# Most gate and up tiles of a feed-forward layer computed with the weights stationary and x moving

## What is computed

```python
def swiglu(x, w_gate, w_up, w_down):
    return (jax.nn.silu(x @ w_gate) * (x @ w_up)) @ w_down

x = layer_norm(alpha * x + 0.5 * swiglu(x, ffn_w_gate[l, 0], ffn_w_up[l, 0], ffn_w_down[l, 0]),
               ln_g[l, 0], ln_b[l, 0])
...
h = h + 0.5 * _swiglu(_rmsnorm(h, ffn_norm[layer, 0]), ffn_w_gate_up[layer, 0], ffn_w_down[layer, 0])
```

## Time and profile before

| | us |
|---|---|
| median of 3 runs (lowest, highest) | 1726.74 (1725.92, 1729.38) |
| the profiled execution | 1726.31 |
| its span, first to last instruction | 1724.6 |
| PE busy in it | 1666.2 |
| DVE busy | 966.6 |
| ACT busy | 746.5 |

### The profile page before, as it was taken

One profiled execution on the slowest core, in us unless ns is written; L12 is line 12 of the kernel. 1 busy time (PEld: TensorE's weight loads), 2 busy tenths in 40 slices (PEclk: granted clock), 3 DMA queues, 4 the chain that ended last, 5 costly groups with the idle time before them and its releaser, 6 DMA issues.

```text
span 1724.6 us, 19555 instructions
## 1 busy us (share of the span) xinstructions
PE 1666.2 (97%) x8230; PEld 1393.8 (81%) x8230; DVE 966.6 (56%) x1016; ACT 746.5 (43%) x910; POOL 32.5 (2%) x53
## 2 busy tenths in 40 slices
PE   7999999998999999999999999997999989999998
PEld 6888888877788877888898888886888877888887
DVE  5555556867755546555467555464655454555552
ACT  5534344646344424444344444343544343535441
POOL 0000000000000000000000000000000020000000
PEclk9999999989999999999999999998999986999999
DMA  8565483434466555555465665454665450037551
GB/s 270 176 215 196 134 265 126 135 93 140 146 220 200 203 177 164 177 202 191 141 228 161 196 188 198 165 174 156 209 193 196 164 171 1 1 109 223 182 194 73
DMA packets 226087, 291.11 MB, mean 169 GB/s; under 512 B 10516, under 2 KB 203728, under 8 KB 225872
## 3 DMA queue, kind: packets, MB, share of 16 engines
q1 hardware_dynamic: 226000, 289.87, 51.1%
HBM read 288.78 MB, written 1.05 MB: 168 GB/s over the span
## 4 chain that ended last, share of the span: by engine, by line
PE 81%; DVE 9%; ACT 3%; issue 2%; DMA 2%; POOL 1%; SPq 0%; DVEq 0%; POOLq 0%; ACTq 0%
PE bank L1532 24%; PE bank L1534 24%; PE bank L1533 24%; DVE w_lo L979 3%; PE bank L1991 2%; PE bank L1693 2%; ACT w_hi L637 1%; PE bank L1541 1%; PE bank L2016 1%; POOL stats L582 1%; DVE z_sb L1041 1%; DVE x_sb L1012 1%; PE bank L2001 1%; DMA raw<-in_w_in_dram 1%; DVE bn L1019 0%
## 5 line engine op out<-in xcount | busy, mean ns | idle before, releaser
L979 DVE TENSOR_TENSOR w_lo<-raw,w_hi 128x2048 fp32r<-128x2048 f32 (+1 forms) x268 | 607.9, 2274 | 335.0 <-ACT w_hi L637 333.8
L637 ACT ACTIVATE w_hi<-raw 128x2048 fp32r<-128x2048 f32 (+1 forms) x268 | 507.7, 1901 | 194.5 <-DMA raw<-in_ffn_w_down_dram 97.2
L1532 PE MATMUL bank<-w_hi,xT_lo 128*128 128x512 f32 (+1 forms) x1360 | 541.2, 398 | 16.9 <-DVE w_lo L979 7.2
L1534 PE MATMUL bank<-w_hi,xT_hi 128*128 128x512 f32 (+1 forms) x1360 | 532.2, 391 | 0.0
L1533 PE MATMUL bank<-w_lo,xT_hi 128*128 128x512 f32 (+1 forms) x1360 | 531.6, 391 | 0.0
L1532 PEld LDWEIGHTS bank<-w_hi,xT_lo 128*128 128x128 f32 x1360 | 258.5, 190 | 70.5 <-issue 10.2
L1534 PEld LDWEIGHTS bank<-w_hi,xT_hi 128*128 128x128 f32 x1360 | 258.0, 190 | 54.4
L1533 PEld LDWEIGHTS bank<-w_lo,xT_hi 128*128 128x128 f32 x1360 | 258.7, 190 | 50.2
L1532 PE MATMUL bank<-w_hi,hT_lo 128*128 128x512 f32 x528 | 206.4, 391 | 0.0
L1534 PE MATMUL bank<-w_hi,hT_hi 128*128 128x512 f32 x528 | 205.6, 389 | 0.0
L1533 PE MATMUL bank<-w_lo,hT_hi 128*128 128x512 f32 x528 | 205.4, 389 | 0.0
(11 more groups left out here) (249 smaller groups left out, 1248.5 us busy)
## 6 DMA issues: line engine op xcount, KB each, us to landing
raw<-in_ffn_w_gate_up_dram SPq DMA_DIRECT2D x176, 512.0 KB, 4.9
raw<-in_ffn_w_down_dram SPq DMA_DIRECT2D x132, 512.0 KB, 4.0
raw<-in_ffn_w_gate_dram SPq DMA_DIRECT2D x44, 512.0 KB, 4.0
raw<-in_ffn_w_up_dram SPq DMA_DIRECT2D x44, 512.0 KB, 5.0
raw<-in_w_in_dram SPq DMA_DIRECT2D x44, 512.0 KB, 4.9
raw<-in_conv_w_in_dram SPq DMA_DIRECT2D x24, 512.0 KB, 4.7
raw<-in_kv_w_dram SPq DMA_DIRECT2D x12, 512.0 KB, 4.3
raw<-in_w_out_dram SPq DMA_DIRECT2D x8, 512.0 KB, 3.6
```

The source lines that it names most:

```text
L637: nc.scalar.activation(w_hi[:, slot, 0:width], raw[:, slot, 0:width], ACT.Copy).then_inc(high_ready, 1)
L979: nc.vector.tensor_tensor(w_lo[:, slot, 0:width], raw[:, slot, 0:width], w_hi[:, slot, 0:width].bitcast(F32), ALU.subtract).then_inc(low_r ...
L1532: nc.tensor.matmul(o, x_lo, wh, start=first, stop=False, skip_group_check=shared)
L1534: return nc.tensor.matmul(o, x_hi, wh, start=False, stop=last_one, skip_group_check=shared)
```

## The change

In the first three tiles (phases 0 and 7) or two tiles (other phases) of each feed-forward layer nothing but places and banks changes. In the other 8 or 9 tiles the roles of the operands are exchanged. `xT_hi` and `xT_lo` become the two halves of one tensor `xT`, so that for each chunk both parts of x are 512 adjacent columns. `features(j, kh)` first runs 16 matmuls of 512 columns (4 chunks x 4 blocks of 128 features) with a high weight stationary and both parts of x moving, after a wait on `high_ready`; then 16 matmuls of 256 columns with a low weight stationary and the high part of x moving, after a wait on `low_ready`. The four blocks (two gate, two up) have a bank each, four banks a tile, by turns. A bank's left half collects x_hi by w_hi and w_lo, its right half x_lo by w_hi. The two halves are joined outside PE: ACT copies the right halves into `silu` and `h` (four copies of 128x256), DVE adds the left halves (four adds). ACT takes Silu in place (one instruction of 512 columns), DVE multiplies (one of 512), ACT writes `hT_hi` and DVE `hT_lo`, both from `h`, which already has features on the partitions. There is no `hidden` for these tiles. PE waits on `up_joined` for its banks.

Tensors and helpers:

```diff
-xT_hi = sb("xT_hi", [P, KC, S], F32R)
-xT_lo = sb("xT_lo", [P, KC, S], F32R)
+xT = sb("xT", [P, KC, 2, S], F32R)
+xT_hi, xT_lo = xT[:, :, 0, :], xT[:, :, 1, :]
...
+FEATURES = [[bank[i] for i in (0, 1, 4, 5)], [bank[i] for i in (2, 3, 6, 7)]]
...
+def token_tiles(n):
+    return 3 if n == 0 or behind_kv(n) else 2
+token_before = [sum(token_tiles(m) for m in range(n) if phases[m] == FFN) for n in range(len(phases))]
+joined_before = [FT * ffn_number[n] - token_before[n] for n in range(len(phases))]
+def hidden_bank(n, j):
+    return bank[4 + j % 2] if token_tiles(n) == 3 else bank[6 + j]
```

ACT:

```diff
-    act.wait_ge(hT_psum, FT * f + j + 1)
+    act.wait_ge(hT_psum, token_before[n] + j + 1)
     nc.scalar.activation(hT_hi[:, 2 * j:2 * j + 2, :],
-                         bank[4 + j % 2][:].rearrange("p (c m) -> p c m", c=2),
+                         hidden_bank(n, j)[:].rearrange("p (c m) -> p c m", c=2),
                          ACT.Copy).then_inc(hT_high, 1)
+def feature_tile(j):
+    before, done = FT * f + j, joined_before[n] + j - token_tiles(n)
+    split_to(s0 + 2 * j + LEAD)
+    act.wait_ge(slab_used, s0 + 2 * j + 2)
+    act.wait_ge(h_ready, 2 * before)
+    for fb in range(2):
+        nc.scalar.activation(silu[:, fb, :], FEATURES[j % 2][fb][:, S:2 * S], ACT.Copy).then_inc(low_half, 1)
+    act.wait_ge(hT_ready, before)
+    for fb in range(2):
+        nc.scalar.activation(h[:, fb, :], FEATURES[j % 2][2 + fb][:, S:2 * S], ACT.Copy).then_inc(low_half, 1)
+    split_to(s0 + 2 * j + 1 + LEAD)
+    act.wait_ge(gate_joined, done + 1)
+    nc.scalar.activation(silu[:], silu[:], ACT.Silu).then_inc(silu_ready, 2)
+    act.wait_ge(h_ready, 2 * before + 2)
+    nc.scalar.activation(hT_hi[:, 2 * j:2 * j + 2, :], h[:], ACT.Copy).then_inc(hT_high, 1)
 def tile(j):
-    if j > 0:
+    if 0 < j <= token_tiles(n):
         hidden(j - 1)
+    if j >= token_tiles(n):
+        feature_tile(j)
+        return
     split_to(s0 + 2 * j + LEAD)
     act.wait_ge(slab_used, s0 + 2 * j + 2)
...
     tile(j)
 for d in range(FC // 2):
-    if d == 1:
-        hidden(FT - 1)
```

DVE:

```diff
 evacuate_input(0)
 split_to(LEAD - 1)
-def small_parameters():
+def small_columns():
     dve.wait_ge(cols_psum, 1)
     nc.vector.tensor_copy(cols[:, 0:ROWS], bank[7][:, 0:ROWS]).then_inc(cols_ready, 1)
     dve.wait_ge(cols_ready, 1)
+def small_parameters():
...
     nc.vector.tensor_tensor(hT_lo[:, 2 * j:2 * j + 2, :],
-                            bank[4 + j % 2][:].rearrange("p (c m) -> p c m", c=2),
+                            hidden_bank(n, j)[:].rearrange("p (c m) -> p c m", c=2),
                             hT_hi[:, 2 * j:2 * j + 2, :].bitcast(F32),
                             ALU.subtract).then_inc(hT_ready, 1)
+def feature_tile(j):
+    done = joined_before[n] + j - token_tiles(n)
+    split_to(s0 + 2 * j + LEAD)
+    for fb in range(4):
+        part, joined = ((silu, gate_joined), (h, up_joined))[fb // 2]
+        dve.wait_ge(low_half, 4 * done + fb + 1)
+        ins = nc.vector.tensor_tensor(part[:, fb % 2, :], FEATURES[j % 2][fb][:, 0:S], part[:, fb % 2, :], ALU.add)
+        if fb % 2 == 1:
+            ins.then_inc(joined, 1)
+    dve.wait_ge(up_joined, done + 1)
+    dve.wait_ge(silu_ready, 2 * FT * f + 2 * j + 2)
+    nc.vector.tensor_tensor(h[:], silu[:], h[:], ALU.mult).then_inc(h_ready, 2)
+    dve.wait_ge(hT_high, FT * f + j + 1)
+    nc.vector.tensor_tensor(hT_lo[:, 2 * j:2 * j + 2, :], h[:], hT_hi[:, 2 * j:2 * j + 2, :].bitcast(F32),
+                            ALU.subtract).then_inc(hT_ready, 1)
+    split_to(s0 + 2 * j + 1 + LEAD)
 def tile(j):
-    if j > 0:
+    if 0 < j <= token_tiles(n):
         hidden(j - 1)
+    if j >= token_tiles(n):
+        feature_tile(j)
+        return
     split_to(s0 + 2 * j + LEAD)
+    if behind_kv(n) and j == 2:
+        keys_out(1, 6)
     for tt in range(NT):
         dve.wait_ge(silu_ready, 2 * FT * f + 2 * j + tt + 1)
...
 if n == 0:
     small_parameters()
 for j in range(3, FT):
     tile(j)
 for d in range(FC // 2):
-    if d == 1:
-        hidden(FT - 1)
     if d < FC // 2 - tail(n):
```

PE:

```diff
         pe.wait_ge(hT_ready, FT * f + j - 1)
-    dst = bank[4 + j % 2][:].rearrange("p (c m) -> p c m", c=2)
+    dst = hidden_bank(n, j)[:].rearrange("p (c m) -> p c m", c=2)
     for c in range(2):
         for tt in range(NT):
             ins = nc.tensor.transpose(dst[:, c, tt * P:(tt + 1) * P], h[:, tt, c * P:(c + 1) * P], ident[:])
     ins.then_inc(hT_psum, 1)
+def features(j, kh):
+    k = s0 + 2 * j + kh
+    hi, lo = slab_view(k % SLOTS, 4, 512)
+    pe.wait_ge(high_ready, k + 1)
+    for c in range(4):
+        x = xT[:, 4 * kh + c, :, :].rearrange("p a m -> p (a m)")
+        for fb in range(4):
+            at, o = slice(fb * P, (fb + 1) * P), FEATURES[j % 2][fb]
+            nc.tensor.matmul(o[:], hi[:, c, at], x, start=kh == 0 and c == 0, stop=False, skip_group_check=True)
+    pe.wait_ge(low_ready, k + 1)
+    for c in range(4):
+        for fb in range(4):
+            at, o = slice(fb * P, (fb + 1) * P), FEATURES[j % 2][fb]
+            ins = nc.tensor.matmul(o[:, 0:S], lo[:, c, at], xT_hi[:, 4 * kh + c, :], start=False,
+                                   stop=kh == 1 and c == 3, skip_group_check=True)
+    ins.then_inc(slab_used, 1)
 def tile(j):
-    gate_up(j, 0)
-    hidden(j - 1)
-    gate_up(j, 1)
+    turned = token_tiles(n)
+    if j < turned:
+        gate_up(j, 0)
+        hidden(j - 1)
+        if behind_kv(n) and j == 2:
+            pe.wait_ge(cmp_ready, 2)
+            transpose_keys(1, 6)
+        gate_up(j, 1)
+        return
+    if j == turned + 1:
+        pe.wait_ge(hT_ready, FT * f + j - 1)
+    if j >= turned + 2:
+        pe.wait_ge(up_joined, joined_before[n] + j - turned - 1)
+    if j == 3 and n == 0:
+        pe.wait_ge(cols_ready, 1)
+    if j == 3 and behind_kv(n):
+        pe.wait_ge(keys_ready, 2)
+    features(j, 0)
+    if j == turned:
+        hidden(j - 1)
+    features(j, 1)
...
-    if behind_kv(n) and j == 2:
-        pe.wait_ge(cmp_ready, 2)
-        transpose_keys(1, 6)
-if n == 0:
-    pe.wait_ge(loaded_rows, 16 * 9)
-    nc.tensor.transpose(bank[7][:, 0:ROWS], z_sb[0:ROWS, 0, 0:P], ident[0:ROWS, 0:ROWS]).then_inc(cols_psum, 1)
+    if n == 0 and j == 1:
+        pe.wait_ge(loaded_rows, 16 * 9)
+        nc.tensor.transpose(bank[7][:, 0:ROWS], z_sb[0:ROWS, 0, 0:P], ident[0:ROWS, 0:ROWS]).then_inc(cols_psum, 1)
 for j in range(3, FT):
     tile(j)
-if n == 0:
-    pe.wait_ge(cols_ready, 1)
-if behind_kv(n):
-    pe.wait_ge(keys_ready, 2)
-project(n, s0 + 2 * FT, FC // 2, hT_hi, hT_lo, lambda d: pe.wait_ge(hT_ready, FT * f + d + 1),
-        behind_first=lambda: hidden(FT - 1))
+pe.wait_ge(up_joined, joined_before[n] + FT - 1 - token_tiles(n))
```

More of the change, by code:

```diff
@@ L268, in two_block_kernel @@
         hT_psum = sem("hT_psum")
+        low_half = sem("low_half")
+        gate_joined = sem("gate_joined")
+        up_joined = sem("up_joined")
         hT_high = sem("hT_high")
@@ L1514, in _ @@
                             keys_out(0, 7)
-                        if behind_kv(n) and j == 2:
-                            keys_out(1, 6)
+                        if n == 0 and j == 1:
+                            small_columns()
                     if n == 0:
@@ L1735, in _ @@
                             transpose_keys(0, 7)
-                        if behind_kv(n) and j == 2:
-                            pe.wait_ge(cmp_ready, 2)
-                            transpose_keys(1, 6)
-                    if n == 0:
-                        pe.wait_ge(loaded_rows, 16 * 9)
-                        nc.tensor.transpose(bank[7][:, 0:ROWS], z_sb[0:ROWS, 0, 0:P], ident[0:ROWS, 0:ROWS]).then_inc(cols_psum, 1)
+                        if n == 0 and j == 1:
+                            pe.wait_ge(loaded_rows, 16 * 9)
+                            nc.tensor.transpose(bank[7][:, 0:ROWS], z_sb[0:ROWS, 0, 0:P], ident[0:ROWS, 0:ROWS]).then_inc(cols_psum, 1)
                     for j in range(3, FT):
                         tile(j)
-                    if n == 0:
-                        pe.wait_ge(cols_ready, 1)
-                    if behind_kv(n):
-                        pe.wait_ge(keys_ready, 2)
-                    project(n, s0 + 2 * FT, FC // 2, hT_hi, hT_lo, lambda d: pe.wait_ge(hT_ready, FT * f + d + 1),
-                            behind_first=lambda: hidden(FT - 1))
+                    pe.wait_ge(up_joined, joined_before[n] + FT - 1 - token_tiles(n))
+                    project(n, s0 + 2 * FT, FC // 2, hT_hi, hT_lo, lambda d: pe.wait_ge(hT_ready, FT * f + d + 1))
                 if kind == MIXER:
```

## The result

| | before | after |
|---|---|---|
| median (lowest to highest), 15 executions each | 1727.06 (1724.69 to 1732.94) | 1720.81 (1709.18 to 1726.76) |
| the profiled execution | 1726.31 | 1713.39 |
| its span | 1724.6 | 1711.7 |
| its mean granted clock | 0.976 | 0.977 |

The change makes the kernel faster: after takes 0.9949 of the time of before, 95% interval 0.9933 to 0.9964. The medians are 6.3 us apart; the forecast was 11.0, for a time of 1715.7 in a range of 1709 to 1724.

A forecast was written before the change was run, and what follows sets the result against it. The prediction took PE to bound the kernel in the gate and up part: -25.0 for transposes, +10.9 for longer slabs, +3.1 for changes of form, -11.0 in all. That gave a median of 1715.7 us, range 1709 to 1724.

The forecast's parts named there:

- The bound: Gate and up part of the FFNs: a microsecond of PE work is a microsecond of time, and nothing else is.
- Removed transposes: Turned gate and up tiles lose the four `hidden` transposes: 52 x 0.48 = 25.0 us saved on PE.
- The longer slab: Each of 104 turned slabs has eight more matmuls and loads, 5.545 against 5.440 us: 10.9 us added.
- the change of form: Going from 256-column to 512-column matmuls, once per turned slab, costs 0.03 us: 104 x 0.03 = 3.1 us added.
- Rival B: Turned slabs: no cost for going from 256 to 512 columns, so -14.1 us, 1712.6; chance 0.20.
- The sum: Over 52 turned tiles: -25.0 + 10.9 + 3.1 = -11.0 us, 0.21 per tile, period 11.15.
- The waits at nothing: PE's new or moved waits, and the phase 7 transposes moved into tile 2, stay hidden: taken as nothing.
- DVE's chain: In a turned tile, from ACT's first copy to DVE's last split: +10.3 us, inside 11.15 with 0.85 over.
- Rival D: Turned tiles: DVE's chain takes PE's place; at 13.5 us a tile, 57 us more, 1773; chance 0.04.
- Rival F: Turned slabs: weight loads using all rows stand in the open, 832 more costing 158 us, 1863; chance 0.01.
- Rival E: Clock behind PE's pauses: half-clock stretches of about 3.5 us; three more give 1726, one fewer 1712; chance 0.08 against gain.

The follow-up runs named there:

- r2_by_chunk: Changed kernel with high and low weight passes alternating chunk by chunk in each slab, PE waiting for the low part ahead of the slab: 1718.17 us, ratio 0.9944.
- r4_longer_dve_chain: Changed kernel with an unused DVE reduction of 2048 columns ahead of each low part in a turned tile, two a tile: 1753.79 us, ratio 1.016.
- r9_more_filled: Changed kernel with constant matmuls in three PE pauses plus three more groups (26 at the start, 12 and 8 later): 1708.79 us, ratio 0.9888.
- r6_look: Changed kernel as it is, one more profiled execution: 1712.5 us at a mean clock of 0.976.
- r8: Kernel before with three groups of constant matmuls in PE's pauses, its new gate and up form left out: 1712.22 us, ratio 0.9903.
- r10: Kernel before with three groups of constant matmuls in PE's pauses, the kernel of r8 once more: 1713.29 us, ratio 0.9914.
- r7_fill_pauses: Changed kernel with constant matmuls in three PE pauses (16, 28 and 16), results unused: 1700.45 us, ratio 0.9845.
- r11_after_filled_pair: The kernel of r7_fill_pauses once more, on one chip with the kernel of r10: 1698.72 us, ratio 0.983.

## Why the prediction was right, and where it was off

**The bound.** PE alone set the time in the gate and up part, before and after. Right: the chain of after holds nothing but PE, and its gain is there in all six layers.

**Removed transposes, 0.48 each time, 25.0 us.** Right to 3%: put back, they cost 0.465 in the chain, 24.2 us, and 24.7 over the six layers.

**The longer slab, 10.9 us, and the change of form, 3.1 us.** A slab was forecast at 5.545 + 0.03 = 5.575 and takes 5.565. The pitches read in the key and value phase held in this mix. The change of form costs 0.02 rather than 0.03 (r2_by_chunk). Together 13.0 us instead of 14.0. That it is not zero, as Rival B had it, is shown by r2_by_chunk; B's sum (-14.1) puts the profiled execution at 1712.2, nevertheless nearer to the 1713.39 than the forecast's 1715.3.

**The sum.** -11.0 forecast, -12.2 in the layers, -12.9 in the span. With the two added terms at 13.0 instead of 14.0 the sum is -12.0, which nearly closes the difference; with the transposes at the 24.2 or 24.7 that they cost when put back it is -11.2 or -11.7, so up to 1 us of the layers' gain stays unassigned. The profiled execution was forecast at 1715.3 and took 1713.39.

**The waits at nothing.** Right: `up_joined`, `cols_ready`, `keys_ready` and the transposes moved in phase 7 show nowhere among PE's waits.

**DVE's chain.** The forecast of +10.3 was right (+10.14), but Rival D's condition was wrong: it took the length of a chain with waits in it for DVE's period. Had DVE been the bound, most of those waits would have gone, and r4_longer_dve_chain shows 8.1 us of need a tile. D was further off than the 0.85 us of room suggested, and its price was too high for the lengthening tried: two reductions cost 41 us, not 137.

**The page's rule (Rival F).** A load of 190 ns stands in the trace for each of 3328 matmuls of the turned tiles, half of them with 256 columns, and none is in the open: the low pass takes 1.91 for sixteen loads and matmuls. The rule stands in the Trainium skill, "TensorE: Matmul & The Clock Gate", in the section "The mechanism", not in the one that the prediction names: a load overlaps matmuls in flight only if the row group differs. Every load here uses all rows, and this case's traces disagree with the rule in that form. The same section also names a load into a background weight buffer as one that is pulled ahead, which the prediction left out; the traces fit that, but no run here shows such a buffer.

**The clock (Rival E, 0.08).** Here the prediction was off. It gave one stretch of half clock more or less as 1712 to 1719, and the median came out 5.1 us above the forecast; 10 of 15 executions had a mean clock lower by about 0.006 and were about 8 us longer. Run again, the same kernel was in the shorter group in 7 of 8. None of the 15 executions lies between 1714.24 and 1718.36, where the forecast of 1715.7 stood: the median is inside the range because the range took in part of E, which is luck as far as the sum goes, and the chance of E was too small. That stretches of half clock begin behind pauses of PE is shown for those in the traces. Where the longer executions have theirs stays open: no profile fell on one.

## What to carry to other kernels

Where PE is the bound, price a new order by the distance from start to start of the same instruction form elsewhere in the trace, and count each change of form once; three such terms gave the gain in the six layers to 10%. To judge whether an engine behind PE takes over, do not take the length of its chain for its need: its waits for a third engine shrink when it is late (here from 2.94 to 0.89 us a tile). And look at the clock behind each pause of PE: constant matmuls in three pauses gave as much as the whole change did, and beside it, but each group must stand in a pause or it costs its own length (2.6 us for the twelve of r9_more_filled).

## What the runs showed of the hardware that was not expected

**The clock falls behind the same pause in one execution and not in another.** In after, PE pauses for 1.88 us ahead of a layer's input, and then its matmuls start 0.43 apart for a while:

```profile
455.51 1.87 PE L1596 MATMUL bank<-ident,x_sb 128*128 128x128 f32 x8 [1.88 <-DVE x_sb L1064]
457.03 0.78 PE L1587 MATMUL bank<-w_hi,xT 128*128 128x512 f32 x1
457.60 0.63 PE L1588 MATMUL bank<-w_lo,xT 128*128 128x512 f32 x1
458.03 0.63 PE L1589 MATMUL bank<-w_hi,xT 128*128 128x512 f32 x1
...
459.21 0.39 PE L1589 MATMUL bank<-w_hi,xT 128*128 128x512 f32 x1
459.44 0.40 PE L1587 MATMUL bank<-w_hi,xT 128*128 128x512 f32 x1
```

0.43 for 512 columns is the lower of the two levels, 1.2 GHz; 0.23 at 459.21 is the upper, 2.4 GHz. In before the pause at the same place was 1.89 us, and the matmuls behind it stood 0.23 apart from the second on. r6_look, an execution of the very kernel that after is, shows the same as before. Their rows, before and then r6_look:

```profile
456.69 1.09 PE L1541 MATMUL bank<-ident,x_sb 128*128 128x128 f32 x8 [1.89 <-DVE x_sb L1032]
```

```profile
455.30 1.09 PE L1596 MATMUL bank<-ident,x_sb 128*128 128x128 f32 x8 [1.89 <-DVE x_sb L1064]
```

From 450 to 462 the granted clock was 1.00 in before and r6_look, and 0.86 in after. From the transposes to the layer's first `hidden` it took 24.08 us in before and in r6_look, and 25.73 in after: 1.65 us of the change's gain, lost to the clock. The three traces of the tiles' old form (before, r8, r10) all keep 1.00 there, and six of the eleven of the new form do not; that is too few to tell chance from an effect of the change. Elsewhere the clock fell the other way (the attention 126.95 in before, 125.20 in after). The same is seen between r7_fill_pauses and r11_after_filled_pair, again one kernel: both pause for 2.2 us (until 1187.55 and 1189.23), and only in r11 do matmuls 0.43 apart follow. This is r11's row for a stretch in which r7 had 1.00:

```profile
1160.00:1210.00 50.00, 45.68 (x230) 36.30 (x230) 29.72 (x41) 25.75 (x32) 1.66 (x3) 0.93 0.57 180
```

The Trainium skill, "TensorE: Matmul & The Clock Gate", section "What's actually happening", says that the number of slow matmuls at a kernel's start varies from run to run. These rows show the same behind a pause inside a kernel, where the number goes down to none.

**Four matmuls of 256 columns behind ones of 512 took 0.47 to 0.48, no more than 4 x 0.1199, and four of 512 behind ones of 256 about 0.02 us more than 4 x 0.2267.** Both were measured with weights loaded for each matmul (r2_by_chunk).
